# Router logits of a mixture of experts computed with stationary router weights, with zeroed banks, context sums and third parts moved

## What is computed

```python
def hier_moe(h, wg, bg, we, be, w_gate, w_up, w_down):
    t = h.reshape(B * L, D)
    p_group = jax.nn.softmax((t @ wg + bg).astype(F32), axis=-1)
    p_top_g, g_idx = lax.top_k(p_group, 1)
    e_logits = (jnp.einsum('td,gde->tge', t, we) + be).astype(F32)
    e_logits = jnp.take_along_axis(e_logits, g_idx[:, :, None], axis=1)[:, 0]
    p_top_e, e_idx = lax.top_k(jax.nn.softmax(e_logits, axis=-1), TOP_K)
    w_sel = p_top_g * p_top_e / jnp.sum(p_top_e, axis=-1, keepdims=True)
    combine = ...
    for gi in range(N_GROUPS):
        hid = (jax.nn.silu(jnp.einsum('td,edf->tef', t, w_gate[gi]))
               * jnp.einsum('td,edf->tef', t, w_up[gi]) * combine[:, gi, :, None])
        out = out + jnp.einsum('tef,efd->td', hid, w_down[gi])
```

## Time and profile before

| | |
|---|---|
| median of 3 runs | 1971.86 us (1971.58 to 1973.24) |
| the profiled execution | 1971.46 us |
| its span, first to last instruction | 1969.6 us |
| TensorE busy | 1868.5 us (95%) |
| VectorE / ScalarE / GpSimd busy | 818.2 / 586.1 / 387.5 us |
| mean granted TensorE clock | 0.978 |
| read from HBM | 427.11 MB |

### The profile page before, as it was taken

How to read it: one execution, slowest core, us unless ns; L and a number is a source line. 1 busy time by engine, 2 the same in 40 slices (tenths; PEclk the granted TensorE clock), 3 DMA queues, 4 the chain that set the end, 5 groups by cost and what they waited for, 6 DMA issues and landing times.

```text
span 1969.6 us, 26164 instructions
## 1 busy us (share of the span) xinstructions
PE 1868.5 (95%) x11248; PEld 1366.6 (69%) x11248; DVE 818.2 (42%) x1342; ACT 586.1 (30%) x892; POOL 387.5 (20%) x205
## 2 busy tenths in 40 slices
PE   5999999999999999999999899999999899889998
PEld 2777796964444343447887657888888688679998
DVE  1615255731111111116343744566655625574333
ACT  2513103331111111113113535223333411544554
POOL 2000000120000000004003132333443210425665
PEclk8999999989999999999999899999999899999999
DMA  9479917669999999992224004454445222414451
GB/s 357 153 256 344 341 44 278 215 270 429 426 427 428 427 427 427 427 394 82 86 86 161 3 33 171 150 181 162 149 150 182 92 91 89 171 47 168 174 196 38
DMA packets 111425, 429.84 MB, mean 218 GB/s; under 512 B 5706, under 2 KB 8821, under 8 KB 98512
## 3 DMA queue, kind: packets, MB, share of 16 engines
q1 hardware_dynamic: 109056, 416.56, 54.5%
q0 software_dynamic: 2256, 11.62, 1.6%
HBM read 427.11 MB, written 1.05 MB: 217 GB/s over the span
## 4 chain that ended last, share of the span: by engine, by line
PE 65%; DMA 17%; DVE 5%; PEld 5%; issue 3%; ACT 3%; POOL 2%; PEldq 0%; SPq 0%; POOLq 0%; DVEq 0%; ACTq 0%
PE bank L556 64%; DMA ring<-in_moe_w_down 7%; PEld bank L556 4%; DMA H<-in_moe_w_down 4%; DMA arena<-in_moe_w_down 4%; DMA ring<-in_ada_w 2%; PE bank L571 1%; PEldq L535 0%; POOL arena L1889 0%; POOL arena L1888 0%; DVE H L1976 0%; DMA ring<-in_w_in 0%; DVE H_low L1983 0%; POOL arena L1893 0%; POOL arena L1891 0%
## 5 line engine op out<-in xcount | busy, mean ns | idle before, releaser
L556 PE MATMUL bank<-arena_r 128*128 128x256 f32 (+1 forms) x2176 | 591.7, 339 | 12.1 <-ACT arena_r L1380 6.1
L556 PE MATMUL bank<-arena_r,ring_low 128*128 128x512 f32 (+2 forms) x1920 | 596.4, 342 | 1.8 <-DVE H_low L1983 1.0
L556 PEld LDWEIGHTS bank<-arena_r 128*128 128x128 f32 x2176 | 384.9, 190 | 63.2 <-issue 18.2
L556 PE MATMUL bank<-arena 128*128 128x64 bf16 (+8 forms) x2908 | 366.1, 319 | 42.7 <-DMA arena<-in_hy_filt_w 11.7
L556 PEld LDWEIGHTS bank<-arena_r,ring_low 128*128 128x128 f32 (+1 forms) x1920 | 352.5, 188 | 47.7 <-issue 2.7
L556 PEld LDWEIGHTS bank<-arena 128*128 128x128 bf16 (+4 forms) x2908 | 206.2, 132 | 203.8 <-issue 168.6
L556 PE MATMUL bank<-H_low,arena_r 128*128 128x512 f32 (+1 forms) x672 | 217.3, 340 | 0.0
L556 PE MATMUL bank<-ring,arena 128*64 128x512 f32 x768 | 172.0, 603 | 8.4 <-DMA ring<-in_moe_w_down 7.9
L2556 DVE SCALAR_TENSOR_TENSOR X<-bank,mod,X 128x256 f32<-128x256 f32 x216 | 94.2, 478 | 196.6 <-PE bank L556 196.6
L1915 POOL TENSOR_TENSOR ring_low<-ring,arena_r 128x2048 fp32r<-128x2048 f32 x31 | 142.3, 4614 | 131.1 <-DVE ring_low L2568 69.1
L1394 ACT ACTIVATE arena<-bank 128x512 f32<-128x512 f32 (+2 forms) x106 | 51.2, 496 | 368.5 <-PE bank L556 368.5
(11 more groups left out here) (304 smaller groups left out, 1845.4 us busy)
## 6 DMA issues: line engine op xcount, KB each, us to landing
ring<-in_w_mlp SPq DMA_DIRECT2D x32, 2048.0 KB, 7.8
ring<-in_w_in SPq DMA_DIRECT2D x26, 2048.0 KB, 9.1
ring<-in_ada_w SPq DMA_DIRECT2D x24, 2048.0 KB, 11.6
ring<-in_moe_w_up SPq DMA_DIRECT2D x17, 2048.0 KB, 23.2
ring<-in_moe_w_gate SPq DMA_DIRECT2D x17, 2048.0 KB, 27.8
arena<-in_moe_w_up SPq DMA_DIRECT2D x15, 2048.0 KB, 22.4
ring<-in_moe_w_down SPq DMA_DIRECT2D x14, 2048.0 KB, 23.3
arena<-in_moe_w_down SPq DMA_DIRECT2D x13, 2048.0 KB, 24.3
```

Of the source, the lines that this page charges most:

```text
L556: ins = nc.tensor.matmul(o, l, r, start=start, stop=stop, skip_group_check=True)
```

## The change

- **Logits.** The 36 columns of router weights of block k are stationary and the 256 tokens of `H` move: 8 products into 36 rows of bank 4, each followed by the transpose of block k for the first half of the tokens. ScalarE copies the 36x256 result to `LGT` (`rt_exp`), two small products with the identity turn it back to tokens by 36, and only then come the 8 transposes of the second half. VectorE waits for `logits` 2.
- **Banks.** The products with `SW` and its memset are gone; the first product of the first pair into each of the four banks has start set instead (`p == 0`).
- **Context sums.** All eight `stat` products stand between `rows(0)` and `rows(1)`. ScalarE copies the gathered tokens before it takes their root.
- **Third parts.** They are formed by VectorE, one ahead of the wait for the exponentials and one while the ranks are formed. The rests of the second half of the tokens (`rest_of(2)`, `rest_of(3)`) now stand there too.
- **Overflow count.** Its maximum is read first, the rest of it is put behind the weights of pair 0.
- **Chunk 7** waits for the sixth `tokens_passed` (the last transpose) in place of `logits`.

```diff
@@ -321,7 +321,7 @@
                 elif c == MRING - 1:
-                    sp.wait_ge(S("logits"), 1)
+                    sp.wait_ge(S("tokens_passed"), 6)
@@ -885,32 +886,27 @@
+            def token(tb, k):
+
+                tr(ps[2 * tb + k // 4][:, (k % 4) * P:(k % 4 + 1) * P], H[:, k, tb * P:(tb + 1) * P], "tokens_passed" if k % 4 == 3 else None)
+
+            pe.wait_ge(S("tables_in"), 64)
+            for k in range(KT):
+                pe.wait_ge(S("normed"), 16 + k + 1)
+                mm(ps[4][0:NR, 0:L], WR[:, k, :], H[:, k, 0:L], k == 0, k == KT - 1, "logits" if k == KT - 1 else None)
+                token(0, k)
+            pe.wait_ge(S("rt_exp"), 1)
             for tb in range(TB):
-                for k in range(KT):
-                    if tb == 0:
-                        pe.wait_ge(S("normed"), 16 + k + 1)
-                    tr(ps[2 * tb + k // 4][:, (k % 4) * P:(k % 4 + 1) * P], H[:, k, tb * P:(tb + 1) * P], "tokens_passed" if k % 4 == 3 else None)
-            pe.wait_ge(S("tables_in"), 64)
-            for tb in range(TB):
-                for k in range(KT):
-                    mm(ps[4][:, tb * NR:(tb + 1) * NR], H[:, k, tb * P:(tb + 1) * P], WR[:, k, :], k == 0, k == KT - 1,
-                       "logits" if (tb, k) == (1, 7) else None)
+                mm(ps[4][:, L + tb * NR:L + (tb + 1) * NR], LGT[0:NR, tb * P:(tb + 1) * P], ident[0:NR, 0:NR], inc="logits" if tb else None)
+            for k in range(KT):
+                token(1, k)
 
             pe.wait_ge(S("selected"), 1)
-            pe.wait_ge(S("h_rest"), 4)
-            for b in range(4):
-                mm(ps[b], SW[:, 0, :], SW[:, 0:4, :], True, False)
-            for k in range(KT // 2):
-                stat(2, k, L, CSQ)
-
-            pe.wait_ge(S("selected"), 2)
...
-            for k in range(KT // 2, KT):
-                stat(2, k, L, CSQ)
@@ -970,7 +966,7 @@
-                        mm(ps[2 * tb + nb], PICK[:, tb * P:(tb + 1) * P], YSh[:, s], False, False)
+                        mm(ps[2 * tb + nb], PICK[:, tb * P:(tb + 1) * P], YSh[:, s], p == 0, False)
@@ -982,6 +978,9 @@
                 rows(u)
+                if u == 0:
+                    for k in range(KT):
+                        stat(2, k, L, CSQ)
@@ -1542,19 +1541,34 @@
+            natural(0)
+            natural(1)
+            act.wait_ge(S("logits"), 1)
+            A_(LGT[0:NR, :], ps[4][0:NR, 0:L], ACT.Copy).then_inc(S("rt_exp"), 1)
+            natural(2)
+            natural(3)
...
+            middle_part(0)
+            router_exp(0)
+            router_exp(1)
+            middle_part(1)
@@ -1858,10 +1872,6 @@
-            for tb in range(TB):
-                pool.wait_ge(S("h_natural"), 4 + tb + 1)
-                i = G.tensor_tensor(HB[:, 2, tb, :], HN[:, tb, :], HB[:, 1, tb, :], ALU.subtract)
-            i.then_inc(S("pool_ready"), 1)
@@ -2212,15 +2222,17 @@
-            V.memset(SW, 0.0).then_inc(S("selected"), 1)
...
+            rest_of(0)
+            rest_of(1)
+            dve.wait_ge(S("logits"), 2)
@@ -2256,7 +2268,14 @@
-            dve.wait_ge(S("rt_exp"), 2)
+            def third_part(tb):
+                dve.wait_ge(S("h_natural"), 4 + tb + 1)
+                return V.tensor_tensor(HB[:, 2, tb, :], HN[:, tb, :], HB[:, 1, tb, :], ALU.subtract)
+
+            rest_of(2)
+            rest_of(3)
+            third_part(0)
+            dve.wait_ge(S("rt_exp"), 3)
@@ -2274,18 +2293,13 @@
             i.then_inc(S("selected"), 1)
+            third_part(1).then_inc(S("pool_ready"), 1)
             dve.wait_ge(S("ranks"), 1)
-            dve.wait_ge(S("selected"), 2)
+            dve.wait_ge(S("selected"), 1)
+            cnt, over = RT[0:1, 300:301], RT[0:1, 301:304]
+            V.tensor_reduce(cnt, ps[5][0:1, 2 * NX:3 * NX], AX.X, ALU.max)
```

More of the change, by code:

```diff
@@ L459, in build @@
         SIL, HID = SILs[0], HIDs[0]
+        LGT = A(5000, L)
         YS = A(7048, D)
@@ L1553, in _ @@
                 square(k, L, CSQ, X[:, :, L:2 * L]).then_inc(S("squares"), 1)
-            for i in range(2):
-                act.wait_ge(S("rt_arg"), i + 1)
-                o = RT[:, 16:24] if i == 0 else RT[:, 200:202]
-                A_(o, o, ACT.Exp).then_inc(S("rt_exp"), 1)
             def gathered_out(e):
@@ L1580, in expert_pair @@
                         gathered_out(2 * p + 4 + u)
+            gathered_out(0)
+            gathered_out(1)
             act.wait_ge(S("sum_ready"), 3)
@@ L2213, in _, with rest_of @@
             norm(1, 0, 1, (0,), False)
-            V.memset(SW, 0.0).then_inc(S("selected"), 1)
             V.memset(RKM[:, :, NX:NX + 4], -1.0)
             V.memset(CMB[:, :, NX:NX + 4], 0.0)
-            for b in range(4):
+            def rest_of(b):
                 dve.wait_ge(S("h_natural"), b + 1)
@@ L2333, in _ @@
             pair_weights(0)
+            for k in range(3):
+                i = V.tensor_scalar(over[:, k:k + 1], cnt, float(CAP * (k + 1)), None, ALU.is_gt)
+            link(i)
+            link(V.tensor_reduce(RT[0:1, 304:305], over, AX.X, ALU.add))
+            V.tensor_copy(npass[0:1, 0:1], RT[0:1, 304:305]).then_inc(S("passes_known"), 1)
             dve.wait_ge(S("gathered"), 2)
```

20 lines of the change are left out of this document (7 added, 13 removed).

## The result

The changed kernel took 1981.82 us (median of 10 runs, 1975.08 to 1986.78) beside 1971.83 us of the kernel before (10 runs, 1968.60 to 1976.49): ratio 1.0045, 95% interval 1.0032 to 1.0057. It is slower, by 10.0 us or, with all runs of both made in this study, by 8.1 us in the mean (1981.07 of 22 runs, 1972.92 of 134). That is under 0.5%, but clear of the noise. The forecast was 1974.7, and its range ended at 1979.4. The profiled execution of the changed kernel took 1976.65 us, with a span of 1974.8.

The account below looks back on a forecast made before the run. The unbroken expert-weight DMA stream, started at the end of `rows(0)`, was taken as the bound. `rows(0)` 0.8 us later plus a 2.0 us hole gave +2.8 us on 1971.46, a median of 1974.7; range 1967.9 to 1979.4, its own 1971.5 to 1976.

Parts of the forecast that it names:

- Step 1: Logits and first transposes: a block takes 0.54 us at full clock, 1.07 at half; the loop ends at 411.9.
- Rival B: Clock stays low through the logits loop; `rows(0)` ends 3.1 to 5.6 us late, about 1978 us in all; chance 0.27.
- Step 2: Turning the logits back to tokens: VectorE begins selection at 413.7, 3.7 us earlier than before.
- Step 3: Selection on VectorE: two rests and a third part add 2.5 us to the chain; ranks start at 422.2.
- Step 4: Ranks: TensorE at half clock after idling, about 1.0 us more; VectorE gets them at 424.6.
- Step 5: Overflow count: 0.76 us leave the chain, a 0.1 step is added; gather starts at about 426.05.
- Step 6: Gather and `rows(0)` partly at half clock: 2.0 us lost; `rows(0)` ends at 437.9, 0.8 us later than before.
- Step 7: Context sums between `rows(0)` and `rows(1)`: 3.4 us on TensorE, a 2.0 us hole in the weight stream at chunk 12.
- Chunk 10: no hole: In the weight stream: chunk 10 is issued 9.55 us after chunk 8, while two chunks take 9.7.
- Step 8: Parts put at nothing: `SW` products apart from their clock effect, memset, GpSimd's third parts, chunk 7, start flags, ScalarE's root.
- After 867 us nothing is changed, and all of it shifts: Behind the last two expert chunks, used at 867.40: no added cost, only the earlier delay carried along.
- Rival E: Worse than Rival B: pairs after the first, each behind by 3.4 us, lose time and open further holes; chance 0.05.

Follow-up runs that it names:

- b2_no_sw: The kernel before without the four `SW` products, start set in the first pair instead; mean 1973.9 us, ratio 0.9997.
- a2_filled: The changed kernel with unread products in TensorE's two waits, five behind the last transpose and two behind the ranks; mean 1976.8 us, ratio 1.0024.
- d1_third_pool: c3_sums_ahead with the first third part on GpSimd again and four context squares made earlier on ScalarE; mean 1975.4 us, ratio 1.0017.
- c2_short: The kernel before without the `SW` products and with one context sum of eight; mean 1979.0 us, ratio 1.0029.
- c3_sums_ahead: The changed kernel with context sums back ahead of the gather, five unread products behind the last transpose and two one-column products; mean 1972.3 us, ratio 1.0000.

## Why the prediction was wrong

**Step 1, the logits loop.** The clock did nearly as foreseen: half for 3.4 us, from 407.4 to 410.8 instead of from 406.1 to 409.5. Rival B did not occur: with transposes making a part of each block the clock came back all the same. The cost of a block was mis-sized: 0.81 us at full clock instead of 0.54, 1.41 instead of 1.07. Two passes of 256 columns and a transpose don't follow each other as in rows of one kind; between the start of the products and that of the transpose lie 0.55 us, and 0.26 more to the next products, where 0.43 and 0.11 were taken.

**Step 2.** VectorE began at 415.79 instead of 413.7: 0.42 us is the later R0, and the other 1.7 are the loop's.

**Step 3.** Right: two rests and a third part were 1.28 and 1.21 us, 2.49 instead of 2.5.

**Step 4.** Right: the half clock was there (7.34 us of waiting ahead of the ranks), and the way from the start of the ranks to VectorE's first step took 2.4 us, as worked out.

**Step 5.** Right in kind; the gather started at 427.95 instead of 426.05, all of it from steps 1 and 2.

**Step 6.** The gather lost 1.4 us at half clock, `rows(0)` 0.1: 1.5 instead of 2.0. `rows(0)` ended at 439.28, 2.2 us later than before, instead of 437.9; 0.4 of it is chance ahead of R0.

**Step 7.** The hole was there, at the place foreseen (205 GB/s in 462 to 464 us) and of 1.6 us instead of 2.0. "Chunk 10: no hole" was nearly right: 348 GB/s in 452 to 456 us, which at 426 is 0.7 us missing.

**Step 8.** No section shows a cost of chunk 7, of the third parts taken from GpSimd or of ScalarE's root. The `SW` products were not nothing for the clock: without them b2_no_sw came to chunk 8 at 34.4 us, 0.8 to 2.1 later than the two profiles of before, as the step allowed for in its clock term.

**The sum up to the end of the experts** was 867.4 + 2.8 = 870.2, and it was 870.99. That is close, with some luck: the loop was sized 1.7 us too short and the losses of steps 6 and 7 together 0.9 too long.

**What failed is the sentence "After 867 us nothing is changed, and all of it shifts".** At the branch 3.2 us were added, and 1.4 more by the half clock behind it: a term of 4.6 us that the sum had at nothing. The instructions on every engine are indeed the same there; their places in TensorE's program are not. The change takes 10 products from TensorE ahead of the branch, and that had to be read as a change of everything behind it that jumps. The earlier trace rows stops at 867.40: the branch, 0.52 us in the trace of before, was never looked at. Rival E, worse than B, named further holes in the pairs; there were none (429.3 + 1.6 accounts for all of them).

**What is left open.** By the sections, the changed kernel loses 1.5 us to chunk 8 (33.8 against 32.3; the two profiles of before differ by 1.3 there), 1.6 to 1.7 in the hole and 4.6 at the branch: 7.7 to 7.8. The means differ by 8.1, with an error of 0.9. So the account closes for this kernel, but it is one of sections from one or two executions against means of many, and for others it closes less well. a2_filled stands 3.9 us over before, where its sections explain 0.8; d1_third_pool 2.5, where they explain 0.3; c2_short stands 6.1 over it, where they add up to 8.6. What the other executions did with the clock can't be seen, and what makes these differences isn't settled. Nor is it shown why the clock is lost or kept ahead of R0.

## What to carry to other kernels

In this kernel, with over 20,000 instructions on TensorE, there was a second cost beside the work: where a branch stands. Whoever adds or removes instructions ahead of a branch that is taken should look at the gap from the branch to its target in both traces, and at the packets of instructions around it, before giving a difference of 3 us to the change itself. And work put on one engine beside another is free only while the two don't exclude each other: GpSimd's third part cost VectorE 1.9 us in d1_third_pool and nothing in the kernel before, where VectorE was waiting.

## What the hardware did that was not expected

- A taken branch over a block of 126 products cost TensorE 0.52 us or 3.5 to 3.9 us, by whether the packet of instructions came 5 us ahead of it or was fetched after it (4141 and 4147 products ahead: long; 4153 to 4159: short). The half clock behind the long one cost 1.4 us more.
- Two identical executions reach the same instruction at 406.2 and 412.9 us, with a granted clock of 0.98 and 0.90 from 230 to 315 us.
- A float32 pass of 256 columns with 36 stationary columns followed by a transpose makes a block of 0.81 us at full clock, where the prediction had worked out 0.21 us for a pass and 0.11 for a transpose from rows in which each followed its own kind.
- A step of VectorE on 16 elements, 0.17 us in c3_sums_ahead, took 2.10 beside GpSimd's subtraction of 1024 elements.
